# Up pieces of the next expert between the down pieces of this one, and the down weights as plain fp32

## The reference

```
hf = rmsnorm(x).reshape(-1, 2048)                  # 288 tokens
for e in range(16):
    gate, up = split(hf @ wu[e], 2)                # wu[e]: 2048 x 1024
    out += combine[:, e:e+1] * ((silu(gate) * up) @ wd[e])   # wd[e]: 512 x 2048
y = rmsnorm(x + out)
```

## Time and profile before

| | |
|---|---|
| median of 3 runs | 1898.47 us (1897.85 to 1899.06) |
| the profiled execution, its time | 1896.4 us |
| its span, first to last instruction | 1894.4 us |
| TensorE busy | 1744.0 us, 92% |
| VectorE busy | 1157.8 us, 61% |
| ScalarE busy | 1059.1 us, 56% |
| mean granted clock of TensorE | 0.973 |
| HBM read | 385.38 MB |

### The profile page before, as it was taken

How to read it: one execution, slowest core, us unless ns; L and a number is a source line. 1 busy time by engine, 2 the same in 40 slices (tenths; PEclk the granted TensorE clock), 3 DMA queues, 4 the chain that set the end, 5 groups by cost and what they waited for, 6 DMA issues and landing times.

```text
span 1894.4 us, 29062 instructions
## 1 busy us (share of the span) xinstructions
PE 1744.0 (92%) x10931; PEld 1518.0 (80%) x10931; DVE 1157.8 (61%) x1442; ACT 1059.1 (56%) x1532; POOL 135.9 (7%) x176
## 2 busy tenths in 40 slices
PE   5999989999999999999999989979898997998895
PEld 5999989999988889888999989965565555665563
DVE  5888874343444444444444454448887787877894
ACT  6676753333344444443333355557877787778773
POOL 2554420000000000000000000000000000000000
PEclk9999989999999999999999999979998998999997
DMA  7565545656545544556655644338897898878892
GB/s 191 145 183 143 151 138 166 177 161 190 149 143 168 169 137 133 150 145 162 173 155 165 192 122 141 146 120 324 350 346 286 318 362 294 342 307 341 324 390 113
DMA packets 418893, 393.56 MB, mean 208 GB/s; under 512 B 19168, under 2 KB 376896, under 8 KB 409664
## 3 DMA queue, kind: packets, MB, share of 16 engines
q1 hardware_dynamic: 407152, 383.04, 61.0%
q10 hardware_dynamic: 10432, 4.79, 0.9%
q0 software_dynamic: 1232, 4.72, 0.9%
HBM read 385.38 MB, written 11.08 MB: 209 GB/s over the span
## 4 chain that ended last, share of the span: by engine, by line
PE 68%; DVE 16%; ACT 8%; issue 5%; POOL 1%; DMA 1%; SPq 0%; ACTq 0%; DVEq 0%; POOLq 0%
PE bank L1095 14%; PE bank L1096 14%; PE bank L1097 13%; DVE sL L1738 8%; PE bank L1445 3%; ACT sH L876 3%; PE bank L1297 2%; PE bank L1300 2%; PE bank L1303 2%; PE bank L1258 2%; PE bank L1259 2%; PE bank L1260 2%; ACT wH L674 2%; PE bank L1310 2%; PE bank L1346 1%
## 5 line engine op out<-in xcount | busy, mean ns | idle before, releaser
L674 ACT ACTIVATE wH<-ring 128x1024 fp32r<-128x1024 f32 x320 | 335.9, 1059 | 541.0 <-PE bank L1097 476.6
L1529 DVE TENSOR_TENSOR wL<-ring,wH 128x1024 fp32r<-128x1024 f32 x320 | 387.9, 1230 | 375.5 <-ACT wH L674 367.4
L1095 PE MATMUL bank<-hH,wH 128*128 128x288 f32 x1792 | 536.9, 300 | 5.8 <-ACTq L736 2.7
L1096 PE MATMUL bank<-hL,wH 128*128 128x288 f32 x1792 | 530.8, 296 | 0.0
L1097 PE MATMUL bank<-hH,wL 128*128 128x288 f32 x1792 | 530.3, 296 | 0.0
L1738 DVE SCALAR_TENSOR_TENSOR sL<-raw,prm,sH 128x1024 fp32r<-128x1024 f32 x256 | 317.6, 1280 | 109.8 <-ACT sH L876 108.2
L1095 PEld LDWEIGHTS bank<-hH,wH 128*128 128x128 f32 x1792 | 339.1, 189 | 13.0 <-issue 7.0
L1096 PEld LDWEIGHTS bank<-hL,wH 128*128 128x128 f32 x1792 | 339.2, 189 | 0.4 <-issue 0.2
L1097 PEld LDWEIGHTS bank<-hH,wL 128*128 128x128 f32 x1792 | 338.9, 189 | 0.0
L876 ACT ACTIVATE sH<-raw,prm 128x1024 fp32r<-128x1024 f32 x256 | 280.9, 1143 | 68.2 <-PE bank L1312 48.0
L1310 PE MATMUL bank<-sH,hgs 128*128 128x512 f32 x512 | 192.6, 459 | 47.5 <-DVE sL L1738 45.2
(11 more groups left out here) (309 smaller groups left out, 2205.5 us busy)
## 6 DMA issues: line engine op xcount, KB each, us to landing
raw<-in_expert_w_up SPq DMA_DIRECT2D x128, 1024.0 KB, 7.2
ring<-in_w_in SPq DMA_DIRECT2D x112, 1024.0 KB, 6.2
raw<-in_expert_w_down SPq DMA_DIRECT2D x64, 1024.0 KB, 7.1
ring<-in_w_pb SPq DMA_DIRECT2D x16, 1024.0 KB, 8.8
ring<-in_w_pa SPq DMA_DIRECT2D x16, 1024.0 KB, 8.8
ring<-in_w_o SPq DMA_DIRECT2D x16, 1024.0 KB, 5.6
cK<-in_cache_k SPq DMA_DIRECT2D x16, 256.0 KB, 2.8
cV<-in_cache_v SPq DMA_DIRECT2D x16, 256.0 KB, 3.3
```

What stands on the lines that cost most here:

```text
L674: a.activation(wH[2 * (slot % 2) + half][:, :, :], ring[slot][:, 8 * half:8 * half + 8, :], ACT.Copy).then_inc(hi_ready, 1)
L1095: pe.matmul(dst, hi, rH[:, k, :], start=(k == 0), stop=False)
L1096: pe.matmul(dst, hi, rL[:, k, :], start=False, stop=False)
L1529: v.tensor_tensor(lo[:, :, :], ring[slot][:, 8 * half:8 * half + 8, :], hi[:, :, :].bitcast(F32), ALU.subtract).then_inc(lo_ready, 1)
```

## The change

The order of the pieces is written as a plan for each expert: U is an up piece of the next expert, D a down piece of this one, and "-" the down pieces that the expert before held back. All down pieces are plain, except the first two of the last expert. `atF` holds all four blocks of the activations, and `atH` and `atL` only the two of the last expert.

```diff
-LEAD = 4
-STREAM = []
-for _e in range(NE):
-    STREAM += [(_e, s) for s in range(LEAD if _e else 0, PU)]
-    if _e + 1 < NE:
-        STREAM += [(_e + 1, s) for s in range(LEAD)]
-    STREAM += [(_e, PU + m) for m in range(PD)]
+PLANS = ["UUUUDUDUDUU", "UU-UDUDUUDUU", "UU-UDUDUUDUU", "UU-UDUDUDUDUU"] * NG
+PLANS[NE - 2] = "UU-UDUUUDUU"
+NATIVE = [(0, 1, 2, 3)] * (NE - 1) + [(2, 3)]
+STREAM = [(0, s) for s in range(PU)]
+_held = []
+for _e in range(NE - 1):
+    _up = _down = 0
+    for _c in PLANS[_e]:
+        if _c == "U":
+            STREAM.append((_e + 1, _up))
+            _up += 1
+        elif _c == "D":
+            STREAM.append((_e, PU + _down))
+            _down += 1
+        else:
+            STREAM += _held
+    _held = [(_e, PU + m) for m in range(_down, PD)]
+STREAM += _held + [(NE - 1, PU + m) for m in range(PD)]
...
+def native(e, s):
+    return s - PU in NATIVE[e]
-SPLIT_T = [t for t in range(HALF_N) if STREAM[t // 2][1] != WHOLE]
+SPLIT_T = [t for t in range(HALF_N) if not native(*STREAM[t // 2])]
+CUT = [e for e in range(NE) if len(NATIVE[e]) < FM]
...
                     old = n - RAW
-                    if STREAM[old][1] == WHOLE:
+                    if native(*STREAM[old]):
                         sp.wait_ge(eh_done, 2 * old + 2)
...
+                        src = pair[e % 2][0][:, 0:FM * CAP].rearrange("p (m c) -> p m c", m=FM)
+                        if e in CUT:
+                            a.activation(atH[:, :, :], src[:, 0:2, :], ACT.Copy).then_inc(atH_ready, 1)
+                        m0 = NATIVE[e][0]
+                        a.activation(atF[:, m0:, :], src[:, m0:, :], ACT.Copy).then_inc(atF_ready, 1)
...
+            def whole(slot, m, half, stop):
+                for c in range(2):
+                    nb = 2 * half + c
+                    ins = pe.matmul(out4[nb][0:CAP, :], atF[:, m, :], raw[slot][:, nb * 512:(nb + 1) * 512],
+                                    start=False, stop=stop, skip_group_check=True)
+                ins.then_inc(eh_done, 1)
...
                 if t == DOWN_AT[e]:
-                    pe.wait_ge(atL_ready, e + 1)
+                    if native(e, s):
+                        pe.wait_ge(atF_ready, e + 1)
+                    else:
+                        pe.wait_ge(atL_ready, NCUT[e] + 1)
...
-                if s == WHOLE:
+                if native(e, s):
                     if half == 0:
+                        pe.wait_ge(atF_ready, e + 1)
                         pe.wait_ge(raw_in[n % RAW], 16 * (n // RAW + 1))
...
+                    whole(n % RAW, s - PU, half, j == EPG - 1 and s == PU + PD - 1)
                     continue
...
-                    if i == AT_AT[e]:
+                    if i == AT_AT[e] and e in CUT:
```

More of the change, by code:

```diff
@@ L52 @@
 PU, PD = KT // 2, FM
-LEAD = 4
 FIRST_LEAD = 3
-STREAM = []
-for _e in range(NE):
-    STREAM += [(_e, s) for s in range(LEAD if _e else 0, PU)]
-    if _e + 1 < NE:
-        STREAM += [(_e + 1, s) for s in range(LEAD)]
-    STREAM += [(_e, PU + m) for m in range(PD)]
+PLANS = ["UUUUDUDUDUU", "UU-UDUDUUDUU", "UU-UDUDUUDUU", "UU-UDUDUDUDUU"] * NG
[16 more added lines that the diff above has]
+STREAM += _held + [(NE - 1, PU + m) for m in range(PD)]
 PIECES = len(STREAM)
 HALF_N = 2 * PIECES
-WHOLE = PU + PD - 1
-SPLIT_T = [t for t in range(HALF_N) if STREAM[t // 2][1] != WHOLE]
+def native(e, s):
+    return s - PU in NATIVE[e]
+SPLIT_T = [t for t in range(HALF_N) if not native(*STREAM[t // 2])]
 NSPLIT = len(SPLIT_T)
 NTH = [sum(1 for x in SPLIT_T if x < t) for t in range(HALF_N + 1)]
+CUT = [e for e in range(NE) if len(NATIVE[e]) < FM]
+NCUT = [sum(1 for x in CUT if x < e) for e in range(NE + 1)]
 UP_AT = [2 * STREAM.index((e, 0)) for e in range(NE)]
@@ L75 @@
 DOWN_AT = [2 * STREAM.index((e, PU)) for e in range(NE)]
-DONE_AT = [2 * (STREAM.index((e, WHOLE)) + 1) for e in range(NE)]
+DONE_AT = [2 * (STREAM.index((e, PU + PD - 1)) + 1) for e in range(NE)]
 TURN_AT = [d - 2 if e + 1 < NE else d for e, d in enumerate(DOWN_AT)]
@@ L321, in build @@
     actHL = sb("actHL", [P, FF], F32R)
-    atH = sb("atH", [P, FM, CAP], F32R)
-    atL = sb("atL", [P, FM, CAP], F32R)
+    atH = sb("atH", [P, 2, CAP], F32R)
+    atL = sb("atL", [P, 2, CAP], F32R)
+    atF = sb("atF", [P, FM, CAP])
     end3 = here[0]
-    here[0] = end3 - (FM + 1) * CAP * 4
-    atF = sb("atF", [P, CAP])
     assert max(end1, end2, end3) <= nc.sbuf_usable_end, (end1, end2, end3, nc.sbuf_usable_end)
@@ L413, in build @@
         actH_ready, actL_ready = sem("actH_ready"), sem("actL_ready")
-        at_ps, atH_ready, atL_ready = sem("at_ps"), sem("atH_ready"), sem("atL_ready")
+        at_ps, atF_ready = sem("at_ps"), sem("atF_ready")
+        atH_ready, atL_ready = sem("atH_ready"), sem("atL_ready")
         sqy_ready, ssqy_ready, rmsy_ready, yo_ready = (sem("sqy_ready"), sem("ssqy_ready"), sem("rmsy_ready"),
@@ L1036, in again @@
                                         a.wait_ge(at_ps, NE + x + 1)
-                                        a.activation(atH[:, :, :],
+                                        a.activation(atF[:, :, :],
                                                      pair[0][0][:, 0:FM * CAP].rearrange("p (m c) -> p m c", m=FM),
-                                                     ACT.Copy).then_inc(atH_ready, 1)
+                                                     ACT.Copy).then_inc(atF_ready, 1)
+                                    if s >= PU:
+                                        continue
                                     a.wait_ge(raw_in[s % 2], 16 * ((PIECES + RAW - 1 - s % 2) // RAW + 6 * x + s // 2 + 1))
@@ L1501, in again @@
                                         ins.then_inc(at_ps, 1)
-                                        pe.wait_ge(atL_ready, NE + x + 1)
+                                        pe.wait_ge(atF_ready, NE + x + 1)
+                                    if s >= PU:
+                                        pe.wait_ge(raw_in[s % 2],
+                                                   16 * ((PIECES + RAW - 1 - s % 2) // RAW + 6 * x + s // 2 + 1))
                                     for half in range(2):
-                                        pe.wait_ge(sL_ready, NSPLIT + 24 * x + 2 * s + half + 1)
                                         if s < PU:
+                                            pe.wait_ge(sL_ready, NSPLIT + 2 * PU * x + 2 * s + half + 1)
                                             k = 2 * s + half
@@ L1509, in again @@
                                         else:
-                                            three([out4[2 * half + c][0:CAP, :] for c in range(2)], atH[:, s - PU, :],
-                                                  atL[:, s - PU, :], sH[half], sL[half])
+                                            whole(s % 2, s - PU, half, False)
                         residual(xsL, False, True).then_inc(ov_end, 1)
@@ L1915, in _ @@
                          .then_inc(actL_ready, 1)
-                    if i == AT_AT[e]:
[L1917 to L1920, removed]
+                    if i == AT_AT[e] and e in CUT:
+                        v.wait_ge(atH_ready, NCUT[e] + 1)
+                        v.wait_ge(atF_ready, e + 1)
+                        v.tensor_tensor(atL[:, :, :], pair[e % 2][0][:, 0:2 * CAP].rearrange("p (m c) -> p m c", m=2),
+                                        atH[:, :, :].bitcast(F32), ALU.subtract).then_inc(atL_ready, 1)
                 for g in range(NG - 1):
@@ L1976, in again @@
                                                         ALU.subtract).then_inc(actL_ready, 1)
[L1977 to L1980, removed]
+                                    if s >= PU:
+                                        continue
                                     for half in range(2):
-                                        v.wait_ge(sH_ready, NSPLIT + 24 * x + 2 * s + half + 1)
+                                        v.wait_ge(sH_ready, NSPLIT + 2 * PU * x + 2 * s + half + 1)
                                         lo(half, s % 2, s, half)
```

## The result

The changed kernel takes 1914.66 us in the median (1913.8 to 1915.2, 4 runs) against 1898.16 us: ratio 1.0087, 95% interval 1.0070 to 1.0105. It is slower by 16.5 us where 20 us less were forecast. The profiled execution has a span of 1912.0 us and a mean granted clock of 0.966.

A forecast was written before the change was run, and what follows sets the result against it. TensorE and VectorE were taken to bound the expert stage in turn, each idling meanwhile. Three groups at 3.9 us (11.7), last group 8.8 and start 0.3 gave 20.8 us off 1898.5: 1878 us, range 1866 to 1893.

The forecast's parts named there:

- DMA, which the sum costs at nothing: Expert-stage fetches: held buffers make them come in bursts of two and three, still landing in time, at no cost.
- the sum: Expert stage: 153.3 us a group against 157.2, last group 101.4 against 110.2, start 0.3; all 20.8 us gained.
- Cover of 1 us there, of 3 in the experts with rounds: Longest burst's third fetch: issued 10.8 us before ScalarE wants it, needs 9.9; 3 us spare in experts with rounds.
- walk through the run: Four up pieces ending an expert's ups: TensorE leaves at 9.6 us against 7.5 at its own pace, waiting 2.2.
- no wait: One or two up pieces between plain ones: VectorE has time enough for its 2.4 or 4.8 us of work.
- the 0.3 us that the sum added to each run: Runs of four up pieces: added because the old order's working gave 21.3 us and its trace 21.6; wait becomes 2.5.
- The change of group: Stretch from one group's finish to the next group's first down product: 23.1 us after, 31.4 before.
- The tail's gap before the last remap: Last group: TensorE's 6.0 us wait for the last activations would be covered by two held plain pieces (6.9).
- (d): Expert-stage fetch bursts land late everywhere: gain gone from 1.6 us an expert, up to 1922 us; chance 0.08.
- (b): TensorE's clock drops at gaps before held plain pieces: 1.6 us each, 18 in all, 1896 us; chance 0.10.
- (c): Last group limited by DMA: 32.7 us an expert at 385 GB/s, some late bursts, 1882 to 1888; chance 0.10.
- (e): More gain: group changes hidden better by 2 us each, or 0.5 us less per run, 1865 us; chance 0.10.

The follow-up runs named there:

- half fetches: The changed kernel, with every expert-stage fetch after the first five bringing only half its bytes (results not the reference's): 1867.01 us, ratio 0.9842.
- six buffers: The changed kernel with six raw buffers instead of five, the final gain left out and the drains unmoved: 1866.31 us, ratio 0.9839.
- early drains: The changed kernel with the drains of the rounds two split indices earlier on ScalarE: 1882.43 us, ratio 0.9922.
- one plain piece: The changed kernel's order, but only each expert's fourth down piece plain and the first three split: 1847.97 us, ratio 0.9740.

## Why the prediction was wrong

**The step that failed** is the one with the words "DMA, which the sum costs at nothing" and "Cover of 1 us there, of 3 in the experts with rounds". It asked of the third fetch of the longest burst whether it lands before its split is wanted, and took the rounds for cover. The piece that decided was another one, the second up piece after an expert's first down piece. It can't be fetched before the held piece's buffer is free, and it isn't TensorE's need of it that matters (it landed at 1416.65 and TensorE came to its products at 1428.70) but a drain that stands behind its splits in ScalarE's order, and for which TensorE's next round waits. The rounds were no cover; they were the victims. The prediction's own walk through the run ended before the drains, and its "no wait" for the stretches with one or two up pieces between plain ones holds only if the pieces have landed. The step also priced its fetches at the 413 GB/s of one window, and from 1408.8 to 1416.7 the core's DMA moved 325. The term at nothing measured 48 us: 1914.66 against 1867.01 with half fetches and 1866.31 with six buffers.

**What the 48 us are made of.** The three groups take 44.3 us more than with half fetches (493.4 against 449.1). TensorE's nine waits for a drain are 25.4 of it. Behind seven of the nine its granted clock is 0.50 to 0.70 in the next 5 us, in which it is busy for 4.9 to 5.0; taken together that is 14 us of its time (an estimate: 5 us times what the clock lacks to 1.00, added up). Behind the waits of 1.96 us (at 1340.64) and 2.58 us (at 1505.40) the clock stays at 1.00. Some 5 us are left without a name.

**What the sum had right, and where it was lucky.** With early drains a group takes 153.5 to 154.7 us against 153.3 in the sum, but that is luck: ScalarE still waits 113.5 us for landings there, and early drains cost 7 us by themselves (1873 against 1866 with six buffers). With half fetches a group takes 149.6, so the sum was 3.7 us too high for each, and 11 us in all: it forecast 1878 for what measured 1866 to 1867. Late landings put 48 us on that. Of the 3.7, the 0.3 us that the sum added to each run isn't in the trace; the rest stays open. The walk through the run of up pieces was right: in the fourth expert TensorE takes 9.5 us (from about 1395.7, 0.93 before the second half's 1396.60, to the held piece at 1405.19), for which it has 9.6; the largest gap in it is 1.2 us, and the rest of the loss is halves at VectorE's pace. The change of group takes 23.7 us in the profile after (1440.4 to 1464.1) against 23.1. A plain piece is 3.43 to 3.45 us, as the sum had it; 3.69 is borne out by no row. That doesn't speak against four passes: 3.45 us over sixteen passes is 0.216 each, while a piece in twelve fp32r products has 2.77, 0.231 each, and 3.69 took a pass to cost as much as such a product. The tail's gap before the last remap fell from 6.0 to 1.4 us.

**The excess over the forecast**: three groups 10.8 + 12.3 + 10.4 = 33.5 us, the last group 2.3, and 1.8 at the first residual; 37.6 against 37.0 measured between the medians. The 1.8 isn't the change's: the stage's first up product already starts at 1265.32 where it started at 1263.28 before, and with early drains it starts at 1263.23.

**The rivals.** (d) had the sign and the cause (the in-order queue and the held buffers) but the wrong price: it needed landings beyond 12 us, and the median is 7.3, the longest 13.9; a landing of 7 to 8 us was enough, since the issue was late. (b), the clock, is real but elsewhere: the lower level comes behind the waits at the rounds and not at the held pieces (1.00 from 1400 to 1410, with the 1.2 us gap in it), and it goes with the waits (with early drains the granted clock from 1298 to 1415 us is 1.00, where the changed kernel has 0.96 from 1300 to 1430); its 14 us are an estimate, no run changed it alone. (c) had the last group bounded by DMA's rate. It took 103.7 us against 101.4 in the sum, but 99.9 with six buffers and the same bytes, so there too it is the time of issue and not the rate. (e), 1865, is what the kernel takes once the landings are in time, and for its reason in part: the sum was too high.

**Where the expected gain was.** The order gives more than was forecast of the whole change: 49 us with one plain piece. The further plain pieces take back 19 us of it even with half fetches (1867 against 1848), and 48 more by holding their buffers.

## What to carry to other kernels

When a consumer works on landed data in place, its buffer is held until that engine is through: follow the in-order queue to the one fetch that waits for it, and then ask what stands behind that piece in the program of each engine that touches it, not only when the piece itself is needed. Small steps that another engine waits for (drains, copies of activations) belong ahead of work that can be late; but ahead of work that is always ready they cost as much, so their place has to be chosen again whenever the stream changes. Before giving up a split to save a slower engine's time, try the order alone: here it was all of the gain.

## What the runs showed that I had not expected

- The place of a 1 us drain is worth 32 us one way and 37 us the other (1914.7 to 1882.4; 1848.0 to 1884.6), with no work changed.
- DMA's mean rate over the stage says nothing of the waits for it. It was 318 GB/s after (1300 to 1870 us) against 332 before (1300 to 1860), and yet DMA was busy for 0.93 to 0.99 of three of ScalarE's waits (at 1333.6, 1371.7 and 1411.1). The idle time lay behind the bursts, and the same bytes with six buffers took 48 us less.
- TensorE's time is lost twice by such a wait: after 3.63 us idle, the next 5 us ran at the lower level, with 1.05 us for a pair of products instead of 0.63.
